# A chunked delta-rule recurrence in a three-block network: two fewer passes in the triangular inverse, the token shift moved to the projection, and one mask operation per chunk

## The reference, cut to what matters

```
prev = jnp.pad(ya, ((0, 0), (1, 0), (0, 0)))[:, :-1]
ya = ya + mu * (prev - ya)                       # the token shift
r, k, v, wd, ad, gd = jnp.split(ya, ...)
...
def step(state, inp):                            # over 512 tokens
    sa = jnp.einsum('bhij,bhj->bhi', state, -kk_t)
    state = (state * w_t[:, :, None, :] + sa[..., :, None] * (kk_t * a_t)[:, :, None, :]
             + v_t[..., :, None] * k_t[:, :, None, :])
    return state, jnp.einsum('bhij,bhj->bhi', state, r_t)
```

## Time and profile before

| | |
|---|---|
| median of three runs | 3592.63 us (3591.66 to 3595.71) |
| the profiled execution | 3596.05 us |
| its span | 3594.2 us, so 1.85 us lie around it |
| busy share of the span | PE 94%, PEld 51%, DVE 32%, ACT 16% |
| mean granted TensorE clock | 0.955 of full speed |
| projection of the second block, pairs | about 1495 to 1617 us |
| attention | about 1638 to 1697 us |
| token shift | 1689.6 to 1705.7 us |
| within the chunks | 1752 to 1786.5 us |
| inverse, group 1 and group 2 | 1786.5 to 1849.6 and 1849.6 to 1913.5 us |

### The profile page before, as it was taken

The page is one execution under the profiler, slowest core; times in us unless marked ns, Lnnn a source line. Parts: engine busy times, 40 slices in busy tenths (PEclk is TensorE's granted clock), DMA queues, the critical chain, the costliest instruction groups (busy, mean ns, idle before and its releaser), DMA issues.

```text
span 3594.2 us, 33790 instructions
## 1 busy us (share of the span) xinstructions
PE 3362.9 (94%) x13834; PEld 1838.4 (51%) x13834; DVE 1165.5 (32%) x2245; ACT 564.5 (16%) x1111; POOL 1.4 (0%) x6
## 2 busy tenths in 40 slices
PE   7999889999999999997698899999889999999998
PEld 4554444333333333583597468854334444468543
DVE  2046531111111111536542254410333594164101
ACT  2033220010000100203310220100313102020000
POOL 0000000000000000000000000000000000000000
PEclk9999999999999999997596899999989999999999
DMA  5122249999999999420000112221210211122220
GB/s 228 47 94 77 111 167 417 428 429 428 429 429 429 429 429 429 183 81 1 0 1 1 47 71 94 75 90 70 73 47 24 94 70 70 70 79 85 73 91 24
DMA packets 41086, 585.17 MB, mean 163 GB/s; under 512 B 4689, under 2 KB 4689, under 8 KB 5393
## 3 DMA queue, kind: packets, MB, share of 16 engines
q1 hardware_dynamic: 40752, 582.45, 39.9%
q0 software_dynamic: 224, 1.18, 0.1%
HBM read 581.51 MB, written 2.10 MB: 162 GB/s over the span
## 4 chain that ended last, share of the span: by engine, by line
PE 83%; DMA 8%; DVE 5%; ACT 3%; issue 1%; SPq 0%; DVEq 0%; ACTq 0%
PE PS L241 26%; PE PS L337 14%; PE PS L1130 10%; DMA ring<-in_weights 8%; PE PS L1110 4%; PE PS L538 3%; PE PS L277 3%; PE PS L721 3%; PE PS L1064 2%; PE PS L1887 2%; PE PS L1588 2%; PE PS L1097 1%; PE PS L678 1%; PE PS L1875 1%; PE PS L544 1%; PE PS L1046 1%
## 5 line engine op out<-in xcount | busy, mean ns | idle before, releaser
L241 PE MATMUL PS<-A,ring 128*128 128x512 f32 x1608 | 703.3, 599 | 26.9 <-DVE A L2232 11.8
L241 PEld LDWEIGHTS PS<-A,ring 128*128 128x128 f32 x1608 | 307.7, 192 | 418.9 <-issue 387.4
L1130 PE MATMUL PS<-A 128*64 128x512 f32 x1280 | 294.0, 601 | 2.3 <-DMA A<-in_weights 0.3
L337 PE MATMUL PS<-A 128*128 128x256 f32 x1056 | 235.1, 379 | 0.0
L241 PE MATMUL PS<-H,ring 128*128 128x512 f32 x544 | 234.1, 592 | 0.0
L337 PEld LDWEIGHTS PS<-A 128*128 128x128 f32 x1056 | 200.6, 190 | 27.3
L1110 PE MATMUL PS<-ring,A 128*64 128x512 f32 x768 | 172.9, 597 | 16.9 <-DMA ring<-in_weights 16.7
L1202 DVE TENSOR_TENSOR A<-A,PS 64x512 f32<-64x512 f32 x64 | 44.1, 690 | 420.9 <-ACT A L1159 420.9
L1130 PE MATMUL PS<-ring,A 128*64 128x512 f32 x768 | 175.4, 598 | 0.8 <-DMA ring<-in_weights 0.5
L1130 PEld LDWEIGHTS PS<-A 128*64 128x64 f32 x1280 | 85.1, 137 | 176.9 <-issue 168.8
L1505 DVE COPY H<-PS 128x512 f32<-128x512 f32 x32 | 22.1, 692 | 455.9 <-ACT A L1524 455.9
(11 more groups left out here) (422 smaller groups left out, 3623.2 us busy)
## 6 DMA issues: line engine op xcount, KB each, us to landing
ring<-in_weights SPq DMA_DIRECT2D x178, 2048.0 KB, 14.0
A<-in_weights SPq DMA_DIRECT2D x96, 2048.0 KB, 24.0
X<-in_x SPq DMA_DIRECT2D x1, 2048.0 KB, 10.3
out_y<-X SPq DMA_DIRECT2D x4, 512.0 KB, 2.6
con<-in_const SPq DMA_DIRECT2D x1, 1423.0 KB, 5.9
vec<-in_vec SPq DMA_DIRECT2D x1, 1075.0 KB, 14.5
A<-in_ctx SPq DMA_DIRECT2D x1, 1024.0 KB, 12.3
con<-in_levels POOLq DMA_DIRECT2D x1, 896.0 KB, 9.1
```

The source lines that it names most:

```text
L241: mm = nc.tensor.matmul(bank[:, 0:out_width], weight_tile(name, n), moving(k), start=k == 0, stop=k == k_tiles - 1)
L337: mm = nc.tensor.matmul(pair_bank(p, n), w[:, k, :], x[:, k, :], start=k == 0 and not more, stop=k == 3, skip_group_check=more)
L1130: mm = nc.tensor.matmul(PS[CAP * up:CAP * (up + 1), c % 2, :], XS[:, k, CAP * b:CAP * (b + 1)], w[:, n:n + 4, :].rearrange("p a b -> p (a ...
```

## The change

Four edits.

- **The token shift** of tiles 0 to 10 is done inside the projection's loop, two tiles at the end of each of pairs 4 to 8 and one at the end of pair 9, with a(24) and a(25) for the differences. ACT and DVE wait for all 11 at the start of the RWKV part.
- **One mask operation per (head, chunk)**: the constants "lt" and "le" change places, so that "lt, le" is one run of 256 columns, and one operation of 512 columns applies it twice.
- **The first level is copied.** With the inverse still the identity, level 0's result is the masked N itself. DVE copies it into KX[j] from SBUF, PE transposes N (12 transposes of 128x128 in a group instead of 12 + 24 products), and DVE copies the transpose into BI[j] by its mask. ACT has no part in it.
- **Half of the last level is left out.** Only KX is formed in level 6, so three units of line 1887 and three masked copies in each group go.

```diff
+                for j in (2 * p - 8, 2 * p - 7):          # in the pair loop of second_dve
+                    if 0 <= j < 11:
+                        token_shift_dve(dve, j)
...
             for g in range(2):
-                for n in range(INV_LEVELS):
+                pe.wait_ge(S["inv_start"], g + 1)
+                for j in range(3):
+                    q = inv_count(g, 0, j, 0) - 1
+                    if q >= 5:
+                        pe.wait_ge(S["inv_used"], q - 4)
+                    for c in range(4):
+                        mm = nc.tensor.transpose(PS[:, 3 + q % 5, c * P:(c + 1) * P], SC2[3 * g + j][:, c, 0, :], ident)
+                    mm.then_inc(S["xnx"], 1)
+                for n in range(1, INV_LEVELS):
                     for j in range(3):
-                        pe.wait_ge(S["inv_start"], g + 1)
-                        if n:
-                            pe.wait_ge(S["inv_used"], 2 * (s - 3) + 2)
+                        pe.wait_ge(S["inv_used"], inv_count(g, n - 1, j, 1 if n > 1 else 0))
...
-                        for turned in range(2):
+                        for turned in (0, 1) if n < INV_LEVELS - 1 else (1,):
...
         def rwkv_act(act):
-            act.wait_ge(S["shifted"], 1)
+            act.wait_ge(S["shifted"], 11)
...
-            for s in range(2 * INV_LEVELS * 3):
+            for s in range(2 * (INV_LEVELS - 1) * 3):
...
+        def token_shift_dve(dve, j):
+            cur, t = a(j), a(24 + j % 2)
+            if j >= 4:
+                u = FAST["win2"][0] + (j - 4) // 2 + 1
+                dve.wait_ge(S["c11"], u)
+                dve.wait_ge(S["c21"], u)
+            if j >= 2:
+                dve.wait_ge(S["shifted"], j - 1)
+            nc.vector.tensor_tensor(t[:, 1:], cur[:, :-1], cur[:, 1:], ALU.subtract)
+            link(dve, "dve", nc.vector.tensor_scalar(t[:, 0:1], cur[:, 0:1], -1.0, None, ALU.mult))
+            nc.vector.scalar_tensor_tensor(cur, t, vcol("mu", j), cur, ALU.mult, ALU.add).then_inc(S["shifted"], 1)
...
-                for q, mask in ((0, "lt"), (1, "le")):
-                    v = nc.vector.tensor_tensor(dst[:, q::2, :], src[:, q::2, :],
-                                                ccol(mask, 0, P).unsqueeze(1).to_broadcast([P, 2, P]), ALU.mult)
-                v.then_inc(S["within_out"], 1)
+                mask = ccol("lt", 0, 2 * P).unsqueeze(1).to_broadcast([P, 2, 2 * P])
+                nc.vector.tensor_tensor(pairs(SC2[m // 4][:, m % 4, :, :].rearrange("p q t -> p (q t)")),
+                                        pairs(PS[:, m % 4, :]), mask, ALU.mult).then_inc(S["within_out"], 1)
...
+                for j in range(3):
+                    nc.vector.copy_predicated(as_tiles(a(KX[j])), wide_level(0, 1), SC2[3 * g + j][:, :, 0, :])
+                for j in range(3):
+                    q = inv_count(g, 0, j, 0)
+                    dve.wait_ge(S["xnx"], q)
+                    nc.vector.copy_predicated(as_tiles(a(BI[j])), wide_level(0, 0), as_tiles(PS[:, 3 + (q - 1) % 5, :])
+                                              ).then_inc(S["inv_used"], 1)
+                for n in range(1, INV_LEVELS):
                     for j in range(3):
+                        dve.wait_ge(S["xnx"], inv_count(g, n, j, 1))
                         for turned, dst in enumerate((BI[j], KX[j])):
...
+                            if turned or n < INV_LEVELS - 1:
+                                q = inv_count(g, n, j, turned)
+                                dve.wait_ge(S["inv_used"], inv_count(g, n - 1, j, turned if n > 1 else 0))
+                                nc.vector.copy_predicated(as_tiles(a(dst)), wide_level(n, turned),
+                                                          as_tiles(PS[:, 3 + (q - 1) % 5, :])).then_inc(S["inv_used"], 1)
```

More of the change, by code:

```diff
@@ L112 @@
 CONSTANTS = [
-    ("ident", 128), ("ones", 128), ("ones64", 128), ("le", 128), ("lt", 128), ("future", 128),
+    ("ident", 128), ("ones", 128), ("ones64", 128), ("lt", 128), ("le", 128), ("future", 128),
     ("swap", 128), ("eps", 4), ("invf", 1), ("sgn", 1),
@@ L1824, in three_blocks @@
         SCL = small[:, 408:420].rearrange("p (a c) -> p a c", a=3)
+        INV_ORDER = [(g, n, j, t) for g in range(2) for n in range(INV_LEVELS) for j in range(3)
+                     for t in ((0,) if n == 0 else (1,) if n == INV_LEVELS - 1 else (0, 1))]
+        inv_count = lambda g, n, j, t: INV_ORDER.index((g, n, j, t)) + 1
         def rwkv_tensor(pe):
@@ L1878, in rwkv_tensor @@
                     for j in range(3):
-                        s = (g * INV_LEVELS + n) * 3 + j
-                        pe.wait_ge(S["nx_out"], s + 1)
-                        for turned in range(2):
+                        pe.wait_ge(S["nx_out"], (g * (INV_LEVELS - 1) + n - 1) * 3 + j + 1)
+                        for turned in (0, 1) if n < INV_LEVELS - 1 else (1,):
+                            q = inv_count(g, n, j, turned) - 1
                             if q >= 5:
@@ L1888, in rwkv_tensor @@
                             mm.then_inc(S["xnx"], 1)
-                            q += 1
             pe.wait_ge(S["inv_kept"], 6)
@@ L1984, in rwkv_act @@
                 norm_power(act, PS[:, 4 + p, :], a(34 + p), 64, eps_col=ccol("eps", 1))
-        def rwkv_dve(dve):
[L1988 to L1995, removed]
+        def token_shift_dve(dve, j):
[9 more added lines that the diff above has]
+            nc.vector.scalar_tensor_tensor(cur, t, vcol("mu", j), cur, ALU.mult, ALU.add).then_inc(S["shifted"], 1)
+        def rwkv_dve(dve):
+            dve.wait_ge(S["shifted"], 11)
             for p in range(3):
@@ L2032, in rwkv_dve @@
                 dve.wait_ge(S["within"], m + 1)
-                src = PS[:, m % 4, :].rearrange("p (q t) -> p q t", q=4)
-                dst = SC2[m // 4][:, m % 4, :, :]
-                for q, mask in ((0, "lt"), (1, "le")):
-                    v = nc.vector.tensor_tensor(dst[:, q::2, :], src[:, q::2, :],
-                                                ccol(mask, 0, P).unsqueeze(1).to_broadcast([P, 2, P]), ALU.mult)
-                v.then_inc(S["within_out"], 1)
+                pairs = lambda v: v.rearrange("p (r w) -> p r w", r=2)
+                mask = ccol("lt", 0, 2 * P).unsqueeze(1).to_broadcast([P, 2, 2 * P])
+                nc.vector.tensor_tensor(pairs(SC2[m // 4][:, m % 4, :, :].rearrange("p q t -> p (q t)")),
+                                        pairs(PS[:, m % 4, :]), mask, ALU.mult).then_inc(S["within_out"], 1)
             dve.wait_ge(S["tok"], 9)
             dve.wait_ge(S["levels"], 16)
-            q = 0
             for g in range(2):
                 wide_ident = ident.unsqueeze(1).to_broadcast([P, 4, P])
+                wide_level = lambda n, turned: level(n, turned).bitcast(U32).unsqueeze(1).to_broadcast([P, 4, P])
                 if g:
@@ L2050, in rwkv_dve @@
                 dve.wait_ge(S["inv_start"], g + 1)
-                for n in range(INV_LEVELS):
+                for j in range(3):
[6 more added lines that the diff above has]
+                for n in range(1, INV_LEVELS):
                     for j in range(3):
+                        dve.wait_ge(S["xnx"], inv_count(g, n, j, 1))
                         for turned, dst in enumerate((BI[j], KX[j])):
[L2054 to L2061, removed]
+                            if turned or n < INV_LEVELS - 1:
[3 more added lines that the diff above has]
+                                                          as_tiles(PS[:, 3 + (q - 1) % 5, :])).then_inc(S["inv_used"], 1)
+                dve.wait_ge(S["inv_used"], inv_count(g, INV_LEVELS - 1, 2, 1))
                 for j in range(3):
```

4 lines of the change are left out of this document (1 added, 3 removed).

## The result

The changed kernel takes 3560.15 us (median of 4 runs, 3559.96 to 3562.32) against 3593.06 us for the kernel before (4 runs): a ratio of 0.9909, 95% interval 0.9892 to 0.9926. So the change is worth 28 to 33 us; the forecast was 28.6.

What follows compares the result with a forecast made beforehand. PE, 94% busy, was taken as the bound, alone through the inverse. Gains of 19.6 (inverse), 8.97 (shift) and 0.07 us (masks) sum to 28.6 off the 3592.63 median: 3564.0 us, range 3559 to 3571.

Steps and rivals of the forecast that it cites:

- Shift, old place: Between attention's last ACT copy and the tanh: removing the token shift ends ACT's idle wait, gain 8.97 us.
- Shift, new place: In the projection's pairs: two shifted tiles, 2.90 us, fit in DVE's idle time and PE's slack, cost 0.
- Masks: Masks within the chunks: one 512-column operation for two of 256 saves only at the last one, gain 0.07 us.
- Start of level 1: Inverse, each group: PE's level 1 starts 2.8 us after the group's first PE instruction, waiting for masked copies.
- Clock at the start: Inverse, start of each group: level 1 partly runs at half clock and loses 0.6 us (0.1 to 1.0).
- Levels 1 to 5: Inverse, middle levels: 8.09 us each, five times making 40.45 us, as before.
- Level 6: Inverse, last level: 6.5 us to the copies of line 2063 instead of 9.82, gain 3.3 us per group.
- A: Start of the inverse: transposes leave the clock low, 3.0 us of gain lost, 3567.0 us; chance 0.25.
- B: Six products behind the old shift place meet the higher clock, 1.8 us sooner, 3562.2 us; chance 0.07.
- C: Projection pairs: the moved shift is not all hidden, costing 5 us, 3569.0 us; chance 0.05.
- D: Inverse stays at 1.2 GHz after its broken start, kernel slower at 3655 us; chance 0.02.
- E: After attention: ACT's tanh still waits for something of DVE, 8.97 us stay, 3573.0 us; chance 0.01.

Runs made afterwards that it cites:

- the second: Changed kernel run again, nothing altered, in a second comparison: 3563.19 us against 3591.48 us for the kernel before, ratio 0.9914.
- e1: Kernel before with only the token shift moved, masks and inverse unchanged: 3584.95 us against 3591.48, ratio 0.9978.
- e2: Kernel before with only level 0 copied and transposed, last level whole, shift and masks unchanged: 3577.21 us, ratio 0.9952 to the kernel before.
- e3: Kernel before with only the BI half of the last level left out: 3585.24 us, ratio 0.998 to the kernel before.
- e7: Changed kernel with the token shift crowded, four tiles behind pairs 7 and 8, three behind pair 9: 3568.85 us, ratio 0.9932 to the kernel before.
- e8: Changed kernel with both groups' inverse starts overlapped with the work ahead of them: 3554.85 us, ratio 0.9894 to the kernel before.
- e9: Changed kernel plus one unread dense product of 128 columns ahead of each of the 24 score units: 3595.39 us, ratio 1.0007 to the kernel before.
- e6: Changed kernel plus unread dense products in PE's pause, two ahead of group 1, five ahead of group 2: 3561.4 us, repeated at 3561.27 us.

## Why the prediction was right

The forecast of 3564.0 us lies 3.9 us above the first median and 0.8 above the second, inside its range both times, and the sum of its terms, 28.6 us, is what the touched stages lost in the profile, 28.66 us. The mechanism of every term was borne out; that the sum agrees to 0.1 us is luck. The trace of before was one with a slow stretch in attention, and the inverse of before takes 124.74 us in it and 125.96 in e1's, so the same subtraction with e1's inverse would give 29.9. Step by step:

- **Shift, old place: 8.97 us forecast, 8.95 measured.** The right move was to take ACT's idle time and not DVE's 16 us. The traces of e2 and e3 add that this price moves with the clock: with attention at full speed the gap is 10.05 us and the work behind it 44.98, together 55.03; with the shift gone 46.57. That makes 8.5 us. The prediction had allowed the products behind the shift a gain from the clock; here it is a loss, for the next six products (line 1839 there, 1843 in the changed kernel) took 2.84 us in e2's trace and 4.40 in the changed kernel's.
- **Shift, new place: 0 forecast, 0.01 measured**; the cover of 3.9 us is confirmed by e7.
- **Masks: 0.07 forecast, 0.07 measured.** Hidden but for the last.
- **Start of level 1: 2.8 us forecast, 2.55 measured.** The masked copy from SBUF, for which there was no row, comes every 0.62 us, and the ones from PSUM here every 0.61; I had taken 0.67.
- **Clock at the start: 0.6 us forecast, 0.84 and 1.49 measured.** The mis-sized term: it was put at 0.1 to 1.0 us, and group 2 lies outside. The rise came 4.3 and 5.7 us behind T0, later than the 4.0 I took as the middle of two rows; e2 shows 6.0 and 3.3. Two rows are no range for such a thing.
- **Levels 1 to 5: 8.09 forecast, 8.04 measured.** PE's repeated wait for `inv_start` is gone from each unit, 0.25 us a group that I had not counted. e3, which keeps it, has 8.09 and e2 8.04; that this wait is the cause was not tested by itself.
- **Level 6: 6.5 forecast, 6.43 measured.**

A group from T0 to its last copies comes to 49.99 and 50.67 us, against 50.35: the errors of the terms cancel, within a group and between the two.

**Of the rivals**, A (transposes leave the clock low) is refuted by e2. The sentence of the Trainium skill that goes with it, in "TensorE: Matmul & The Clock Gate", "Part 4: PE-mode transpose", holds that full clock does not engage for transposes, which do not count as busy in the same way; the rise 0.7 us behind the first product speaks against it, and the measurement decides. B: the six products met 1.2 GHz here, where the clock fell 0.6 us ahead of them (at 1696.5), but the rival is a matter of less than a microsecond: in e7 it fell 0.9 us behind their start, they took 5.48 us, and the stage was 0.8 us shorter (45.71 against 46.53). C: not in the change; where e7 forced it, the cover was 4.1 us where the rival had 3.9. D: the clock stood at 1.00 from 1782 on in group 1 and from 1837 in group 2. E: the gap is 0.02 us.

What the forecast lacked was not a mechanism but a width: about 3 us in attention, 2 us in the first chunk and 1 to 1.5 us in either group change between traces in code that no edit touches. The comparison of two medians carries all of it.

## What to carry to other kernels

Price work that moves off a path by the idle time of the engine that waits for it, not by its length, and price its new place by adding up the idle pieces between it and the first instruction that another engine waits for. Where the granted clock changes level, compare stage by stage before asking why a total is 4 us off: the stages that were not touched show how much of it is nobody's doing. Look at such a stretch in the traces of several kernels that share its code: one trace of before had made attention 2.8 us too long. When an iteration starts from the identity, its first step is a copy, and where two such iterations follow one another, the start of the second can lie under the end of the first (e8, 8.5 us for both starts).

## What the runs showed that I had not expected

- Transposes lift TensorE's clock: 3.3 us after twelve transposes began, with 0.7 us of products behind them (e2). They do not always: the burst at 1749.3 in the trace of before, with 64-row products behind it, left the clock at 0.50.
- One dense product in each unit of 64-row products does not lift it, and costs 1.3 us each at 1.2 GHz: 0.7 for itself and 0.6 for what its neighbours no longer overlap, half of that at the five changes of head (e9).
- The same instructions lost 1.6 us at the start of group 1 in one execution and 3.1 us in another (before, e3), by where the clock happened to rise.
- One execution of e6 was 19 us shorter than its fellows; eight others of the same code were not. Its mean granted clock was higher (0.962 against 0.958); in which stage is open.
